# A chunked delta-rule scan on one core: inverse products of two turns issued together on four quarters of the array, and the order of a turn rewritten

## The reference, cut to what matters

```python
def wkv_scan(r, w, k, v, kk, a, s0, reverse):
    def step(S, inp):
        r_t, w_t, k_t, v_t, kk_t, a_t = inp
        sa = jnp.einsum("bhvk,bhk->bhv", S, kk_t)
        S = (S * w_t[:, :, None, :]
             - sa[..., None] * (kk_t * a_t)[:, :, None, :]
             + v_t[..., None] * k_t[:, :, None, :])
        return S, jnp.einsum("bhvk,bhk->bhv", S, r_t)
```

## Time and profile before

| what | before |
|---|---|
| median of 3 runs | 2325.28 us (2323.98 to 2328.12) |
| the profiled execution, its time | 2323.39 us |
| its span | 2321.4 us |
| granted TensorE clock | 1.000 |
| PE busy over the span | 2286.7 us (99%) |
| DVE, ACT, POOL busy | 1585.1, 560.6, 416.3 us |

### The profile page before, as it was taken

One profiled execution on the slowest core, in us unless ns is written; L12 is line 12 of the kernel. 1 busy time (PEld: TensorE's weight loads), 2 busy tenths in 40 slices (PEclk: granted clock), 3 DMA queues, 4 the chain that ended last, 5 costly groups with the idle time before them and its releaser, 6 DMA issues.

```text
span 2321.4 us, 56828 instructions
## 1 busy us (share of the span) xinstructions
PE 2286.7 (99%) x24772; PEld 2015.2 (87%) x24772; DVE 1585.1 (68%) x3256; ACT 560.6 (24%) x1310; POOL 416.3 (18%) x483
## 2 busy tenths in 40 slices
PE   8999999999999999999999999999999999999999
PEld 8999889999999998889999988568888888456558
DVE  7886756888778767568897786446666665147652
ACT  2101050111011000401110201335555554032341
POOL 1111000111111200001122530034444441100000
PEclk9999999999999999999999999999999999999999
DMA  7555454445545554545455322013333334212212
GB/s 283 195 182 187 179 193 169 163 166 183 200 180 183 182 199 152 213 162 182 173 190 182 129 90 73 37 31 63 61 59 60 58 58 101 99 58 88 73 37 73
DMA packets 169462, 310.35 MB, mean 134 GB/s; under 512 B 108992, under 2 KB 134768, under 8 KB 135296
## 3 DMA queue, kind: packets, MB, share of 16 engines
q1 hardware_dynamic: 165024, 278.02, 36.0%
q0 software_dynamic: 4192, 28.72, 3.4%
HBM read 293.06 MB, written 13.63 MB: 132 GB/s over the span
## 4 chain that ended last, share of the span: by engine, by line
PE 93%; DVE 3%; ACT 2%; issue 1%; DMA 1%; SPq 0%; POOL 0%; DVEq 0%; POOLq 0%
PE psum L718 22%; PE psum L1106 22%; PE psum L1167 12%; PE psum L1306 6%; PE psum L736 6%; PE psum L1205 5%; PE psum L1411 3%; PE psum L1400 2%; PE psum L1413 2%; PE psum L1508 1%; PE psum L1504 1%; PE psum L1077 1%; DVE arena L2463 1%; DVE arena L2933 1%; PE psum L1434 1%
## 5 line engine op out<-in xcount | busy, mean ns | idle before, releaser
L718 PE MATMUL psum<-arena,ring 128*128 128x256 f32 (+1 forms) x2288 | 550.6, 399 | 8.1 <-ACT arena L1815 7.8
L718 PEld LDWEIGHTS psum<-arena,ring 128*128 128x128 f32 x2288 | 432.4, 190 | 113.5 <-issue 56.3
L1106 PE MATMUL psum<-arena 128*128 128x128 f32 x2560 | 325.0, 275 | 0.0
L1106 PEld LDWEIGHTS psum<-arena 128*128 128x128 f32 x2560 | 305.1, 192 | 0.0
L1106 PE MATMUL psum<-arena,ring 128*128 128x128 f32 x1920 | 253.6, 275 | 0.0
L1106 PEld LDWEIGHTS psum<-arena,ring 128*128 128x128 f32 x1920 | 233.9, 192 | 0.2
L2441 DVE TENSOR_TENSOR arena<-ring 128x1024 f32<-128x1024 f32 x154 | 192.8, 1252 | 46.1 <-PE psum L1167 34.5
L1167 PE MATMUL psum<-arena 128*128 128x128 f32 x1408 | 184.7, 275 | 0.0
L1167 PEld LDWEIGHTS psum<-arena 128*128 128x128 f32 x1408 | 170.7, 192 | 0.0
L1411 PE MATMUL psum<-arena 64*64 64x64 f32 x2560 | 162.5, 223 | 6.7 <-DVE arena L2933 4.8
L2463 DVE SCALAR_TENSOR_TENSOR arena<-arena 128x256 f32<-128x256 f32 x336 | 164.3, 530 | 5.1
(11 more groups left out here) (351 smaller groups left out, 3622.1 us busy)
## 6 DMA issues: line engine op xcount, KB each, us to landing
ring<-in_weights SPq DMA_DIRECT2D x238, 1024.0 KB, 4.8
arena<-in_ada POOLq DMA_DIRECT2D x24, 1024.0 KB, 5.2
squares<-arena SPq DMA_DIRECT2D x128, 96.0 KB, 2.1
arena<-squares SPq DMA_DIRECT2D x128, 64.0 KB, 2.9
arena<-squares SPq DMA_DIRECT2D x128, 32.0 KB, 2.3
arena<-in_const POOLq DMA_DIRECT2D x1, 1312.0 KB, 6.6
arena<-in_x SPq DMA_DIRECT2D x1, 1024.0 KB, 4.8
ring<-in_weights SPq DMA_DIRECT2D x2, 512.0 KB, 6.5
```

Of the source, the lines that this page charges most:

```text
L718: mm = self.nc.tensor.matmul(out, self.ring[:, slot % RING, i * P:(i + 1) * P], rhs, start=(kc == 0), stop=(kc == len(moving) - 1))
L1106: mm = nc.tensor.matmul(bank[:, n * P:(n + 1) * P], left[:, kind, pair, :], right[:, pair, :], start=(n == 0 and pair == 0), stop=(n == la ...
```

## The change

Five things change, all in the scan.

- For odd turns the two heads swap partitions from level to level (`half_of`): `first_gram` and every inverse product of an odd turn cross from one half to the other, so they use the two quarters off the diagonal. Level 5 ends with each head at home. `lower_product` stays on the diagonal.
- `next_inverses(q, level, level_ahead)` issues the inverse products of turn q at level 4 with those of q+1 at level 1, and at level 5 with level 2, as one alternating sequence behind both masks. `next_inverse(q, 3)` is split in two around `solve(k)`.
- The `lt` matrix of an odd turn is needed in both halves, so ACT copies it across once (`copy_across`, two instructions of 64x256, in even turns), with a semaphore of its own.
- The order on PE: `state_product(k)` heads the turn; "middle" goes behind both lower products and "end" ahead of `solve(k + 1)`; "kv" and `out_and_state(k + 1)` go ahead of the last joint step.
- The order on ACT and DVE: ACT takes the gates (`side_end`) ahead of `take_kv` and takes o ahead of the level 5 inverse; DVE masks (q+1, 1) ahead of `update_state(k)` and (q+1, 2) ahead of `sum_decays` and `update_state(k + 1)`. In `SCAN`, "end" now stands ahead of "kv".

```diff
-PLACES = ("middle", "kv", "end")
+PLACES = ("middle", "end", "kv")
...
+    def half_of(q, level, h):
+        return h if q % 2 == 0 else (h + level) % 2
...
+                        to = halves[half_of(q, 1, h)]
+                        mm_(ps_first[q % 2][to, 0, u, :], alpha, beta, start=True, stop=True)
...
+                held = b * (2 - level % 2)
+                if held == 2:
+                    pe.wait_ge(s.lt_copied, q // 2 + 1)
...
+            def inverse_product(q, level, i, u, h):
+                b, at, to = q % 2, halves[half_of(q, level, h)], halves[half_of(q, level + 1, h)]
+                y_, t_ = xy[at, b, 1, u, :], t_low[at, b, u, :]
+                left, right = (t_, y_) if i else (y_, t_)
+                return mm_(ps_xy[b][to, i, u, :], left, right, start=True, stop=True)
...
+            def next_inverses(q, level, level_ahead):
+                pe.wait_ge(s.t_masked[q % 2], level_count(q, level))
+                pe.wait_ge(s.t_masked[(q + 1) % 2], level_count(q + 1, level_ahead))
                 for u in range(4):
+                    for i in (1, 0):
+                        for h in range(2):
+                            if i or level < LEVELS - 1:
+                                mm = inverse_product(q, level, i, u, h)
+                        for h in range(2):
+                            mm_ahead = inverse_product(q + 1, level_ahead, i, u, h)
+                mm.then_inc(s.xy_full[q % 2], 1)
+                mm_ahead.then_inc(s.xy_full[(q + 1) % 2], 1)
...
+                if k >= 0:
+                    state_product(k)
                 if ahead and q >= 1:
                     first_gram(q + 1)
-                if k >= 0:
-                    state_product(k)
                 lower_product(q, 3)
                 stacked_gram(q)
+                next_inverse(q, 3, range(0, 2))
                 if k >= 0:
                     solve(k)
-                next_inverse(q, 3)
+                next_inverse(q, 3, range(2, 4))
                 if k >= 0:
                     out_and_state(k)
-                side(q, "middle")
                 lower_product(q, 4)
                 if ahead:
                     lower_product(q + 1, 1)
-                next_inverse(q, 4)
+                side(q, "middle")
+                if ahead:
+                    next_inverses(q, 4, 1)
+                else:
+                    next_inverse(q, 4)
                 if k >= 0:
                     state_product(k + 1)
-                if ahead:
-                    next_inverse(q + 1, 1)
-                lower_product(q, 5)
+                side(q, "end")
                 if k >= 0:
                     solve(k + 1)
-                side(q, "kv")
+                lower_product(q, 5)
                 if ahead:
                     lower_product(q + 1, 2)
-                next_inverse(q, 5)
+                side(q, "kv")
                 if k >= 0:
                     out_and_state(k + 1)
-                side(q, "end")
                 if ahead:
-                    next_inverse(q + 1, 2)
+                    next_inverses(q, 5, 2)
+                else:
+                    next_inverse(q, 5)
...
+            def copy_across(q):
+                act.wait_ge(s.inverse_begun[1], q // 2 + 1)
+                for to, of in ((slice(0, HEAD), slice(HEAD, P)), (slice(HEAD, P), slice(0, HEAD))):
+                    ins = nc.scalar.activation(lt_held[2][to, :, :], lt_held[1][of, :, :], ACT.Copy)
+                ins.then_inc(s.lt_copied, 1)
```

More of the change, by code:

```diff
@@ L634, in __init__ @@
         self.s_updated = new("s_updated")
+        self.lt_copied = new("lt_copied")
         self.ones_laid = [new(f"ones_laid_{b}") for b in range(2)]
@@ L880, in build @@
     t_low = second.take(2, 4, CHUNK)
-    lt_all = second.take(2, 4, CHUNK)
+    lt_even = second.take(1, 4, CHUNK)
+    lt_odd = norm_buf.rearrange("p (n u t) -> p n u t", n=2, u=4)
+    lt_held = lt_even[:, 0, :, :], lt_odd[:, 0, :, :], lt_odd[:, 1, :, :]
     y_done = second.take(2, 4, CHUNK)
@@ new lines, in next_inverse @@
+            def next_inverse(q, level, units=range(4)):
+                b = q % 2
+                if units[0] == 0:
+                    pe.wait_ge(s.t_masked[b], level_count(q, level))
+                for u in units:
+                    for i in (1, 0) if level < LEVELS - 1 else (1,):
+                        for h in range(2):
+                            mm = inverse_product(q, level, i, u, h)
+                if units[-1] == 3:
+                    mm.then_inc(s.xy_full[b], 1)
+            def next_inverses(q, level, level_ahead):
+                pe.wait_ge(s.t_masked[q % 2], level_count(q, level))
+                pe.wait_ge(s.t_masked[(q + 1) % 2], level_count(q + 1, level_ahead))
+                for u in range(4):
+                    for i in (1, 0):
+                        for h in range(2):
+                            if i or level < LEVELS - 1:
+                                mm = inverse_product(q, level, i, u, h)
+                        for h in range(2):
+                            mm_ahead = inverse_product(q + 1, level_ahead, i, u, h)
+                mm.then_inc(s.xy_full[q % 2], 1)
+                mm_ahead.then_inc(s.xy_full[(q + 1) % 2], 1)
@@ L2043, in side_middle, with side_end @@
                     exponentials(pair + 1, 0)
-            def side_tail(q):
-                pair, g = divmod(q, GROUPS)
+            def side_end(q):
                 names = scan_tiles(q, "end")
@@ L2050, in side_tail @@
                         take_gates(kind, names[0][1])
+            def side_tail(q):
+                pair, g = divmod(q, GROUPS)
                 if g == 1 and pair + 1 < PAIRS:
@@ L2112, in _ @@
                     take_o(k)
+                if ahead and q % 2 == 0:
+                    copy_across(q + 1)
                 side_middle(q)
@@ L2131, in _ @@
                 side_middle(q)
+                side_end(q)
                 side_tail(q)
@@ L3005, in _ @@
                 if k >= 0:
+                    update_state(k)
+                side_middle(q)
+                if k >= 0:
                     take_z(k + 1)
-                side_middle(q)
                 mask_lower(q, 5)
+                if ahead:
+                    mask_lower(q + 1, 2)
                 if q % GROUPS == 0 and q // GROUPS + 1 < PAIRS:
                     sum_decays(q // GROUPS + 1)
-                if ahead:
-                    mask_lower(q + 1, 2)
-                    turn_squares(q + 1)
                 if k >= 0:
                     update_state(k + 1)
+                if ahead:
+                    turn_squares(q + 1)
             for k in (2 * TURNS - 2, 2 * TURNS - 1):
```

24 lines of the change are left out of this document (7 added, 17 removed).

## The result

The changed kernel takes 2340.31 us (median of 4, 2337.49 to 2341.80) against 2324.91 us; the ratio is 1.0062, 95% interval 1.0045 to 1.0080. The forecast was 2306, with a range up to 2318. The profiled execution took 2341.8 us, its span is 2339.8.

The account below looks back on a forecast made before the run. PE, working on quarters, was taken to bound the scan. In four turns, joint steps -5.6, first Gram -0.3, old waits -3.0 and new waits +6.4 give -2.5 us; times 7.75, -19.4: 2306 us, own range 2297 to 2313, whole range 2286 to 2318.

Parts of the forecast that it names:

- the part at nothing: Items priced at 0 us: ACT's two copies across, and the scan's weight and value DMAs behind the squares.
- the term of the joint steps: On PE, each joint step takes 0.93 us, saving 1.40 us a turn, 5.6 us in four turns.
- C: Rival: records have a floor between starts; at 22 ns -1 us, 2325; by the skill's rule 2334; chance 0.05.
- D: Rival: quarters of one row half take turns in the joint step, no gain there; +26 us, 2352; chance 0.07.
- kv behind the gates, g = 3: New PE wait once in four turns: kv needs the bank that the first w gate empties; 1.5 us.
- mask behind z and the root, g = 3: New PE wait once in four turns: z, then the level 3 mask, come behind ACT's square root; 1.4 us.
- joint step on both masks, g = 2: New PE wait: the joint step of levels 4 and 1 waits for both masks without "middle" as cover; 0.7 us.
- u in the first half, a turn: New PE wait for u, covered only by the split product's second half; 0.27 us each turn, 1.1 in four.
- state product behind the update, g = 0: New PE wait at the turn's head, with two scans of decays ahead of the update on DVE; 0.7 us.
- The old waits: PE's waits for u, for the mask behind the state update and for level 4's mask; all 3.0 us in four go.
- four turns of 55 us or more: Sign: with a joint step of 0.95 us, this would mean undersized waits; about 53.5 us was forecast.
- rival B: The new waits are longer, 8 us in four turns, o, update and state delayed in a row; -7 us, 2318; chance 0.10.

Follow-up runs that it names:

- x2: The changed kernel with DVE's transposed squares moved further ahead, between the second z and the mask of level 5: 2320.59 us, ratio 0.9976.
- z1: y2 plus a one-column Tanh on ACT, result unused, ahead of the joint step's copies in a pair's fourth turn: 2301.83 us, ratio 0.9897.
- w2: z1 with the squares back at the end of DVE's turn, where the change put them: 2325.59 us, ratio 0.9998.
- x1: The changed kernel with the squares back ahead of the second state update: 2327.45 us, ratio 1.0006.
- z2: z1 with both joint steps taken apart into separate inverse products: 2309.15 us, ratio 0.9926.
- w1: The kernel before with only the one-column Tanh of z1 added: 2318.93 us, ratio 0.9974.
- y2: x2 with kv counted ahead of the o_var tile, so z at g = 3 no longer waits for the square root: 2316.32 us, ratio 0.9961.

## Why the prediction was wrong

**The step that failed** is in the part at nothing: "DVE makes it after the update as before, and nothing is moved past it". Before, the squares stood ahead of `update_state(k + 1)`; the change moved the update past them. The transfer was priced at zero without a row for its chain, and no rival named it. With the squares out of the loop, x2 stands 20 us under the changed kernel and z1 24 under w2. That is the sign of the result.

This step is not the whole miss. x1 has the squares where the prediction took them to be, and it came out at 2327.45, no faster than the kernel before. So the step accounts for 13 of the 34 us between 2306 and 2340, and the other 21 lie in the sum, in the term of the joint steps.

**The joint steps** ran at the forecast pace, so C and D fell: 64 records in 0.99 us are one start in 15.5 ns. The Trainium skill (TensorE: Matmul & The Clock Gate, section "Wait — 56ns, not 53.3ns?") has a floor of about 25 ns between starts; the row of 64 records disagrees. But the term was mis-sized. -5.6 us in four turns was the price of the records alone, and issuing them together gives -1.0 (7.3 / 7.75). A joint step denies its neighbours a quarter and waits for the later of two masks, and products taken apart in the new order already overlap at the seams: over z2's turns they take 1.66 and 1.26 us to the next group's start, where the sum had 1.86 and 1.40. This 0.34 us a turn comes with the swap of the halves and stays with the change. An estimate from these numbers closes the sum: 36 us of joint steps that did not come (4.6 x 7.75), less 10.5 that the seams gave (0.34 x 31), plus 13 of the loop, on 2306, make about 2344; 2340 was measured.

**The new waits**, each by its row (a wait's bracket plus 0.16):

| term | forecast | measured |
|---|---|---|
| kv behind the gates, g = 3 | 1.5 | 1.77 (L1484, 1.61) |
| mask behind z and the root, g = 3 | 1.4 | 1.18 (L1423, 1.02) |
| joint step on both masks, g = 2 | 0.7 | 0.78 (z1's row, 0.62) |
| u in the first half, a turn | 0.27 | 0.23 (mean of z1's turns) |
| state product behind the update, g = 0 | 0.7 | 0.42 (z1's waits: 0.3 the longest) |

Each of these was right within 0.3 us. The terms of 0.2 (gates at g = 0), 0.5 (z at g = 2) and 0.3 (first Gram) were not measured singly. The joint step also waits for both masks at g = 1, which the sum had as covered by "middle": z1 starts it 0.56 us later there than z2. **The old waits** were not all gone: what the sum called removed was in part the table's load, which the change only put in another place; w1 takes 6 us out of the old order by itself.

**What the profile after should have shown** was met in its first half (joint steps of 0.95 us, kv on L2040, L1423 behind z). The text then said that four turns of 55 us or more would mean undersized waits, rival B. They took 59.24. But B had no wait for a transfer in it, and its own place, the state product behind the update, cost PE only 0.8 us in four pairs (L1514 behind L3014), against 6.6 for the transfer.

**What stays open.** The granted clock falls below 1 in four stretches of 3.4 us of the changed kernel's scan and one of 6.8 us behind it, and in none of the kernel before but at its very end. They add up to 20.4 us at half pace, so they can have cost up to 10.2. The first, with the row before it:

```profile
1762.00:1766.00 4.00, 2.39 (x75) 2.12 (x75) 0.85 (x2) 3.31 (x7) 2.31 (x2) 0.99 0.25 41
1766.00:1769.00 3.00, 3.00 (x77) 3.00 (x71) 2.23 (x9) 1.87 (x5) 0.00 (x0) 0.50 0.00 0
```

PE was busy for 2.39 of 4.00 us while kv waited, and then the clock stood at the lower of its two levels, 1.2 GHz, for 3.4 us: 48 records took 1.87 us instead of 1.16. The clock does not explain what x2 gained. Its scan has four such stretches too, 13.6 us as in the changed kernel's, and yet its time from the first z to the last is 15.7 us shorter (441.2 against 456.9). Only behind the scan do the two differ in clock, by the 6.8 us, and there by 3.0 us of time. Why the clock falls in some turns and not in others stays open.

## What to carry to other kernels

When a change rewrites an order by hand, walk every queue, SPq's too, and for each transfer ask what now stands ahead of the instruction that starts it: a 10 us round trip through memory is free while it hangs beside the path and sets the pace once its start depends on its own result. A matmul step is worth what the starts of its neighbours move by, not what its own records shrink by. A table load can be drawn forward with a one-column activation into idle time.

## What was not expected of the hardware

- Four quarters of the array keep up one 64-column float32 record in 15.5 ns over 64 records, with two quarters in each row half.
- The round trip of the squares took 7.6 to 10.7 us from the last transpose to the landing of v, though single transfers land in 1.9 to 4.3 us: four issues out and four back, of 0.3 to 2.1 us each, stand in a row on SPq, with a landing after each four. The Trainium skill (DMA: Bandwidth & Descriptors, section "Anatomy of one DMA — SWDGE (gpsimd) path") gives a fixed part of about 2.0 us for a transfer of another kind of queue; the fastest here is near it, and the issues in a row come on top.
- A wait of PE of 1.77 us in a busy stretch was followed by 3.4 us at half clock. y2 has the same wait, in one turn of four, and only one such stretch in its scan, so the wait alone is not enough for it.
